# A two-layer decoder trunk on one core: output chunks every one and a half ticks, VectorE sums one row of each searchless tick, and the last tile joins the sum at half way

## The reference

```python
def hybrid_layer(x, ...):
    h = rmsnorm(x, g_mix)
    z = h @ w_in                                   # p | q | k | v | gate logits
    branch_a = pool_mixer(p, w_pool, pool_scale)   # trailing means over 2, 4, 8, 16 tokens
    branch_b = moba_attention(q, k, v) @ w_attn_up # causal, 8 heads, ALiBi
    merged = gates[..., :D] * branch_a + gates[..., D:] * branch_b
    x = x + merged @ w_out
    return x + peer_ffn(rmsnorm(x, g_ffn), w_peer_q, peer_keys, peer_u, peer_v)

def peer_ffn(x, w_q, sub_keys, u, v):              # for each token and each of 8 heads
    s = einsum('thpd,pkd->thpk', q, sub_keys)      # q = x @ w_q, two halves of 128 keys
    # the 16 best of each half, the 16 best of their 256 sums: 128 experts per token in all
    act = gelu(einsum('thkd,td->thk', u[eid], x))
    return einsum('thk,thkd->td', softmax(best) * act, v[eid])
```

## Time and profile before

| | |
|---|---|
| Median of 3 runs | 1605.27 us (1602.56 to 1605.53) |
| The profiled execution | 1605.11 us |
| Its span, first to last instruction | 1603.3 us |
| TensorE matmuls busy | 1339.2 us (84%) |
| VectorE busy | 1096.5 us (68%) |
| ScalarE busy | 931.9 us (58%) |
| POOL busy | 668.7 us (42%) |
| Bytes moved by DMA | 649.58 MB, 405 GB/s over the span |

### The profile page before, as it was taken

How to read it: one execution, slowest core, us unless ns; L and a number is a source line. 1 busy time by engine, 2 the same in 40 slices (tenths; PEclk the granted TensorE clock), 3 DMA queues, 4 the chain that set the end, 5 groups by cost and what they waited for, 6 DMA issues and landing times.

```text
span 1603.3 us, 18944 instructions
## 1 busy us (share of the span) xinstructions
PE 1339.2 (84%) x5676; PEld 806.5 (50%) x5676; DVE 1096.5 (68%) x2608; ACT 931.9 (58%) x3344; POOL 668.7 (42%) x516
## 2 busy tenths in 40 slices
PE   8997878888987788877898878888988987778876
PEld 7984656644653356653465436655545532223222
DVE  1059978865777877745577887876667877777545
ACT  1216546567755745534775674555675666667766
POOL 0013434355444533424544353334453455455563
PEclk9999999999999998988999999999999999999999
DMA  7779999999999999999999999999999999999997
GB/s 294 291 300 423 422 424 422 423 422 412 388 422 417 415 420 423 422 424 424 420 410 423 418 409 425 422 423 422 375 422 422 421 394 420 422 421 422 415 421 292
DMA packets 91231, 649.58 MB, mean 405 GB/s; under 512 B 10056, under 2 KB 11512, under 8 KB 12536
## 3 DMA queue, kind: packets, MB, share of 16 engines
q0 software_dynamic: 73728, 536.90, 81.0%
q1 hardware_dynamic: 17076, 111.24, 17.0%
q10 hardware_dynamic: 324, 0.23, 0.1%
HBM read 647.28 MB, written 1.05 MB: 404 GB/s over the span
## 4 chain that ended last, share of the span: by engine, by line
DMA 53%; PE 20%; DVE 16%; ACT 5%; issue 5%; POOL 1%; DVEq 0%; ACTq 0%; POOLq 0%
DMA ring<-in_uv,expert 52%; PE ybank L612 10%; DVE ring L1041 7%; PE bank L423 5%; DVE xs L1054 3%; PE bank L561 2%; POOL ring L1172 1%; ACT wgt L787 1%; ACT diag L797 1%; ACT th L785 1%; DVE buf L876 1%; DVE picked L879 1%; ACT arg L782 1%; DMA wring<-in_chunks 1%; ACT sq L779 1%
## 5 line engine op out<-in xcount | busy, mean ns | idle before, releaser
L1172 POOL DMA_INDIRECT ring<-in_uv,expert x512 | 668.5, 1306 | 914.1 <-PE ybank L612 554.8
L612 PE MATMUL ybank<-ring,diag 128*128 128x512 f32 x1664 | 838.2, 638 | 239.7 <-ACT diag L797 234.6
L1041 DVE SCALAR_TENSOR_TENSOR ring<-ring,tok 128x1024 f32<-128x1024 f32 x512 | 625.9, 1224 | 384.3 <-DMA ring<-in_uv,expert 379.5
L612 PEld LDWEIGHTS ybank<-ring,diag 128*128 128x128 f32 x1664 | 303.2, 197 | 682.5 <-ACT diag L797 420.2
L779 ACT ACTIVATE sq<-dots 128x1 f32<-128x1 f32 x512 | 103.1, 201 | 525.5 <-DVE ring L1041 525.1
L423 PEld LDWEIGHTS bank<-hT,wring 128*128 128x128 f32 x2176 | 256.7, 196 | 23.0 <-issue 20.6
L423 PE MATMUL bank<-hT,wring 128*128 128x128 f32 x2176 | 259.0, 279 | 4.0 <-DVE hT L928 2.2
L787 ACT ACTIVATE wgt<-th,half_p 128x1 f32<-128x1 f32 x512 | 198.1, 387 | 17.1
L797 ACT ACTIVATE diag<-cst,wgt 128x128 f32<-128x128 f32 x416 | 167.0, 402 | 13.5
L785 ACT ACTIVATE th<-arg,dots 128x1 f32<-128x1 f32 x512 | 150.8, 295 | 16.6
L782 ACT ACTIVATE arg<-sq,gelu_bias 128x1 f32<-128x1 f32 x512 | 142.9, 279 | 0.0
(11 more groups left out here) (113 smaller groups left out, 735.3 us busy)
## 6 DMA issues: line engine op xcount, KB each, us to landing
wring<-in_chunks SPq DMA_DIRECT2D x84, 1024.0 KB, 9.2
held<-in_chunks SPq DMA_DIRECT2D x18, 1024.0 KB, 21.2
ring<-in_uv,expert POOLq DMA_INDIRECT x512, 12.1
xs<-in_x SPq DMA_DIRECT2D x2, 512.0 KB, 12.5
wpool<-in_w_pool SPq DMA_DIRECT2D x2, 512.0 KB, 13.7
trunk_out<-buf SPq DMA_DIRECT2D x4, 256.0 KB, 4.7
ring<-in_pool_scale SPq DMA_DIRECT2D x1, 512.0 KB, 8.4
cst<-in_consts SPq DMA_DIRECT2D x1, 448.0 KB, 6.0
```

What stands on the lines that cost most here:

```text
L612: ins = pe.matmul(ybank[m][:, :], diag[:, nth % DIAGS, :], ring[:, (2 * t + r) % RING, D + m * BANK:D + (m + 1) * BANK], start=(nth == ten ...
L1041: dve.scalar_tensor_tensor(out=ring[:, g % RING, 0:D], in0=ring[:, g % RING, 0:D], scalar=1.0, in1=tok[:, :], op0=ALU.mult, op1=ALU.mult, ...
L1172: pool.indirect_dma_start(ring[:, g % RING, :], None, uv, bass.IndirectOffsetOnAxis(ap=expert[:, at:at + 1], axis=0)).then_inc(row_landed[ ...
```

## The change

- The four out chunks stand at 31, 32.5, 34 and 35.5 instead of 31 to 34, the queries at 42, 44, ... 56 instead of 41 to 55.
- VectorE sums row 0 also in all mix ticks from 29 to 46 (`EASY`), not only in those with a chunk.
- The steps behind the out chunks move with them: VectorE's adds to 33 + 1.5 n, TensorE's and ScalarE's turns, the squares and the root, the searches by half a tick, and the gain rows from 58 to 59.
- In the last window x goes into `ybank` at tick 32 of its 64 instead of tick 0, on top of the rows summed so far.

```diff
-CHUNK_TICKS = (5, 6, 7, 8, 9, 10, 12, 13, 14, 15, 17, 18, 20, 21, 23, 24, 25, 26, 31, 32, 33, 34,
-               41, 43, 45, 47, 49, 51, 53, 55)
+CHUNK_TICKS = (5, 6, 7, 8, 9, 10, 12, 13, 14, 15, 17, 18, 20, 21, 23, 24, 25, 26, 31, 32.5, 34, 35.5,
+               42, 44, 46, 48, 50, 52, 54, 56)
+
+EASY = range(29, 47)
...
-            return when(w, 46 + (15 if w == windows - 1 else 11) * h // 2 + 2 * step)
+            return when(w, 46.5 + (15 if w == windows - 1 else 11) * h // 2 + 2 * step)
...
-        takes_chunk = {when(w, n) for w in range(1, windows) for n in CHUNK_TICKS} | set(first_queries)
+        shared = {when(w, ceil(n)) for w in range(1, windows) for n in (*CHUNK_TICKS, *EASY)} | set(first_queries)
...
-            return (1,) if t in takes_chunk else (0, 1)
+            return (1,) if t in shared else (0, 1)
...
-            yield when(w, 37)
+            yield when(w, 36.5)
             if w:
                 turn_mixed(0)
+            yield when(w, 38)
             turn_mixed(1)
+            yield when(w, 39.5)
             turn_mixed(2)
...
-                yield when(w, 58)
+                yield when(w, 59)
                 everywhere(pe, w, G_FFN, "gain")
...
-            if last and n == r == 0:
+            if last and n == TICKS // 2 and r == 0:
                 pe.wait_ge(x_mixed, OUTS * windows)
                 for m in range(2):
-                    pe.matmul(ybank[m][:, :], ident, x_of(w % NT)[:, m * BANK:(m + 1) * BANK], start=True, stop=False)
+                    pe.matmul(ybank[m][:, :], ident, x_of(w % NT)[:, m * BANK:(m + 1) * BANK], start=False, stop=False)
...
-                                start=(nth == tensor_rows(w * TICKS) and not last),
+                                start=(nth == tensor_rows(w * TICKS)),
...
             turned(0)
-            yield when(w, 38.5)
+            yield when(w, 39)
             turned(1)
+            yield when(w, 40.5)
             turned(2)
-            yield when(w, 39)
+            yield when(w, 41)
...
-            yield when(w, 41)
+            yield when(w, 43)
             if w == 0:
...
-                yield when(w, 33 + n)
+                yield when(w, 33 + 1.5 * n)
...
-            yield when(w, 40)
+            yield when(w, 42)
```

More of the change, by code:

```diff
@@ L9 @@
 from contextlib import ExitStack
+from math import ceil
 import numpy as np
```

## The result

The changed kernel takes 1609.53 us (median of 7 runs, 1608.1 to 1613.98) against 1604.75 for the kernel before in 7 runs beside it (1602.56 to 1605.53): a ratio of 1.0036, interval 1.0025 to 1.0048. That is slower, by more than the 0.2% that a measurement tells, and 0.03 us outside the predicted range. (The two medians alone stand at 1.0030.) A second measurement gave 1.0043. The forecast was 1603.7. Of the rivals, costly handovers stood at 1609 to 1612.8 and the cold clock at 1607.8.

The account below looks back on a forecast made before the run. Transfers at about 422 GB/s were taken to bound the kernel, with dips where TensorE releases rows late. Terms -7.5 + 5 + 1 + 0 = -1.5 us on 1605.27 gave 1603.7; range 1595 to 1609.5, the forecast's own 1600 to 1606.

Parts of the forecast that it names:

- costly handovers: Rival: the new window's first sum is over 4 us late at 64 too, chunks not covering; 1612.8 or 1609; chance 0.17.
- the cold clock: Rival: each matmul series begins at half clock, so 6 of the middle's 9.7 us stay; 1607.8; chance 0.08.
- The middle: Dips between handovers, 9.7 us, from TensorE late in ticks 34 to 50; relief leaves 2: -7.5 us (-9.7 to -3.5).
- The handovers: Ticks 64, 128, 192: later gain rows, last query and searches delay the new window: 0, +5 and +1 us.
- +5 at tick 128: Gain-bank wait and half search delay the close; first issue near 916 instead of 911.04; bounds 0 to 7.
- +1 at 192: Moving the ident matmuls gives about 3 us, the later last query eats it; bounds -2.6 to +3.
- 0 at 64: First row as late as at 128, but SyncE's three chunk loads fill the hole; bounds 0 to +5.
- The order of events at 128: Gain banks full, `tok`, dot, half search, dot, close at 913.8, then TensorE's first sum and POOL's issue near 916.
- its sum for 192: Last query to 1263.8, gains until 1277, close until 1281.5, first row 1283.3, issue near 1283.8.
- The rival of full cost: The costly handovers rival, chance 0.17: decides as soon as two handovers issue 5 us late.
- The ident matmuls: Moved to tick 224, with 1 us to spare: 0, at most +0.5; taken out at 192, about 3 us gained.
- The signs named ahead: Profile after: x127, 1532 matmuls, three quiet middle stretches, `tok` waiting 2 to 5 us, POOL waiting 8 to 9, slow rows.

Follow-up runs that it names:

- b_easy: Kernel before with only VectorE summing row 0 also in mix ticks 29 to 46: 1602.55 us against 1603.29, ratio 0.9993.
- a_gain58_search46: Changed kernel with gain rows back at mix tick 58 and searches half a tick earlier: 1602.33 us against 1602.85 for the kernel before, ratio 0.9997.
- both of before: Two profiles of the unchanged kernel before: the original one (execution of 1605.11 us) and one more run for its profile alone, 1602.9 us.
- b_ident: Kernel before with only the last tile joining TensorE's sum at tick 32 of its window instead of tick 0: 1602.84 us, ratio 1.0005.
- a_gs_noeasy: Changed kernel with gain rows at 58, searches half a tick earlier and VectorE's new rows taken away: 1602.69 us against 1603.29 before, ratio 0.9997.
- b_gain55: Kernel before with the gain rows at mix tick 55, behind the score of head 6, instead of 58: 1604.87 us against 1603.15, ratio 1.0013.
- a_gs_query41: Changed kernel with gain rows at 58, searches half a tick earlier and queries back at 41 to 55: 1602.52 us against 1603.29 before, ratio 0.9997.
- b_easy_ident_gain55: Kernel before with VectorE's rows in ticks 29 to 46, the ident part and gain rows at 55: 1603.83 us against 1603.15, ratio 1.0005.
- b_easy_warm: Kernel before with VectorE's rows in ticks 29 to 46 and eight zero-weight matmuls in five mix ticks: 1602.12 us against 1603.23, ratio 0.9994.
- after_again: The changed kernel once more, unchanged: 1609.86 us against 1603.23 for the kernel before, ratio 1.0043.
- a_search46: Changed kernel with only the searches moved back half a tick earlier: 1605.37 us against 1602.85 for the kernel before, ratio 1.0011.
- a_gain58: Changed kernel with only the gain rows back at mix tick 58: 1603.56 us against 1602.85 for the kernel before, ratio 1.0003.

## Why the prediction was wrong

**The middle: this term failed.** Predicted -7.5 us (-9.7 to -3.5). VectorE's rows alone (b_easy) brought -1.1 us (-2.6 to +0.2), and all that is left of the change when the handovers are mended (a_gain58_search46) -0.5 (-1.9 to +1.0); both lie outside the bounds. The step that was wrong is to book the dips of three places of one profile as time. The two worst do go quiet: 370:430 moves 411 to 421 GB/s in every profile with VectorE's rows and 392 to 409 in those without.

The middle as a whole is another matter. It has 9.7 us of dips on average over the three profiles with the old stream there (both of before, and b_ident) and 4.4 in the two of the change, but 6.6 in b_easy, 9.3 in a_gain58_search46 and 4.3 to 8.0 in the other eight with VectorE's rows. A loss turns up ahead of tick 192 besides: 1240:1280 loses 1.0 to 4.1 us in every profile with VectorE's rows, and 0.1 to 0.5 in both of before, b_ident and a_gs_noeasy (b_gain55 has 1.9 without them).

**The handovers: about right in time, too small and in the wrong places by the dips.** The prediction put +5 at tick 128, +1 at 192 and 0 at 64. Undoing the two steps that delay the close takes 6.3 to 7.4 us off the change (1.0036 or 1.0043 against 0.9997). By the dips (before 1.5, 1.6 and 0.8, where 192 is without b_ident; after 7.2, 6.9 and 1.9) the handovers cost 5.7, 5.3 and 1.1: **+12.1 in place of +6**. With -5.3 in the middle that makes +6.8, where the measured medians say +4.8 and +6.6. So in time the miss lies in the middle, and that +6 comes near is in part luck, since 192 was put at +1; in the dips of the change itself the handovers miss by 6 and the middle by 2. The two accounts differ because the dips of the middle come back when the handovers are mended. The terms don't add as the sum took them to.

- *The order of events at 128 was right, the time by luck.* `tok` waited 3.63 us for the gain rows, the close ended at 912.7 (predicted 913.8), the issue came at 916.79 (predicted 916): a close 1.1 us earlier than written and a first row 1.8 us slower all but cancel. The price was a little too small: POOL waited 11.35 us, where "8 to 9" was written, and at this tick each of the last microseconds costs a whole one.
- *Left out: the first row after the close is a cold one.* TensorE idles 6.53 us for the close. In 912:917 its granted clock is 0.53, in 1283:1288 0.50, the lower of its two levels (1.2 and 2.4 GHz) nearly all the time, and from its start to the first issue it takes 916.79 - 912.74 = 4.05 us (4.06 at tick 64, 4.05 at 192). At 192 of b_ident, after 1.82 us of idle time, it takes 2.26. That is 1.8 us more at each handover. The prediction looked for the cold clock in the middle and not here, and its sum for 192 used the warm 1.8 us of a row. The Trainium skill (TensorE: Matmul & The Clock Gate, Loop structure matters more than you think) says that a long wait between matmuls makes those behind it run cold; at the three handovers of the change, with 4.45 to 6.53 us of waiting, the trace agrees each time.
- *At 192 the chain was longer than its sum.* The sum moved the last query alone, but all of them move: the seventh now stands where the last one stood, at 1253.01, and starts cold with its score (L590 1.06 us instead of the 0.61 of the earlier trace rows, L425 4.49 instead of 3.74). The last one runs from 1262.94 and ends at 1266.7, not 1263.8; the close ends at 1283.8, not 1281.5; the first issue is at 1287.90, not 1283.8. Of these 4.1 us 2.3 lie ahead of the close (some 1.5 of them only because this execution had lost more by then, 12.9 us of dips against 11.4) and 1.8 in the cold first row.
- *And a loss ahead of the handover.* POOL waits 5.92 us at 1259.50, and 1250:1280 loses 4.1 us before the handover has begun, 2.0 in the second profile. The later queries aren't shown to be the cause: with the queries on their old ticks 1240:1280 loses 2.6 us in a_gs_query41 and 4.0 in b_easy_ident_gain55.
- *At 64 the cover held.* The wait at POOL is 11.35 us as at 128, and 500:510 moves 425 GB/s, since the chunk loads lie there. The rival of full cost was wrong in this, and right that both the others issue 5 us late and decide the sign.

**The ident matmuls.** Costed at nothing in tick 224 and as part of the +1 at 192; b_ident shows their move to cost -0.6 to +2.2 us (its interval, of 1602.85), no gain. The prediction counted a dip of 2.6 us of one profile as something to be had, and the 3.33 us of two cold matmuls as what their move gives: in the second profile of the kernel before the first issue comes 3.97 us after TensorE's start, in b_ident 2.26, so it gives 1.7.

**The signs named ahead.** x127, x1532, the slow rows and the wait for the gain rows ahead of `tok` came as listed, at 192 with 6.77 us instead of 2 to 5. Two of the three stretches of the middle are quiet; that of ticks 97 to 115 is not (2.0 us of dips in 740:880, and 1.3 before). POOL's wait of 8 to 9 us was 9.27 to 11.35.

**What stays open.** That the gain rows at tick 59 and the half search make the change slower is shown: without them it takes the time of the kernel before. Why the middle's relief buys next to nothing is not. The sum of the dips is 11 to 14 us in every kernel whose gain rows don't stand at tick 59, whichever part was moved, 16 with the search at 46, and 20 to 21 in the change. Something gives back in one place what is won in another; the clock of five ticks (b_easy_warm), the spacing (a_gs_noeasy), the query ticks (a_gs_query41) and the ident matmuls (b_ident) were each tried and are not it alone. Nor is it settled why gain rows at tick 55 cost 0.1%.

## What to carry to other kernels

Where a step moves by half a tick in a cyclic plan, look first at the points where one round hands over to the next: write down what each engine does there in strict order, and add to the length of the chain the slow clock of the engine that was kept waiting. In this kernel, bound by transfers and with some rows of reserve, lateness at tick 128 cost little up to some 4 us of waiting and its full length beyond. And don't book a dip of a single profile as a gain: run the same kernel twice and see whether it stands in the same place, and change the one part alone before its term goes into a sum.

## What the runs showed of the hardware

- In the change TensorE, after waiting 4.45 to 6.53 us, starts at a granted clock of 0.50 to 0.55 (over 5 us), and the first row's issue comes 4.05 us after its start instead of 2.26. All ten such starts after 4.45 us or more (after, after_again, a_search46, and tick 128 of a_gain58) took 3.68 to 4.06. After shorter waits both come: at tick 128, 3.41 us of waiting went with 3.84 us in a_gain58_search46, and 3.42 with 2.26 in a_gs_noeasy.
- A single row of 1.98 us took 3.78 in b_easy with gaps of 1.19 and 1.66 us ahead of it (granted clock 0.64 to 0.67 over 10 us); eight small matmuls ahead of it brought 1.98 back after a gap of 1.07.
- The same instruction stream has its dips elsewhere from one execution to the next: 0.7, 0.2 and 3.5 us at tick 128, 2.8 and 0.4 at tick 192. The slow case has the slower matmuls each time: 3.78 us for the gain rows at 128 instead of 2.05 and 2.42, 3.33 for the ident matmuls at 192 instead of 1.98.
